# A two-block layer: the first round's four experts gathered in four column groups, the residual kept in column order, and the first expert's membership found ahead of the routing

## What is computed

```python
hn = rmsnorm(h, norm_ffn)
g_logits = tokens @ w_router_group;  g_idx = argmax(g_logits)            # 4 groups
e_sel = e_logits[g_idx];  top_v, top_i = lax.top_k(e_sel, 2)             # 2 of the group's 8 experts
gates = g_w * softmax(top_v)
ys = (silu(xb @ w_gate[e]) * (xb @ w_up[e])) @ w_down[e]                 # blocks of tokens of one expert
out = zeros.at[row_token].add(ys * row_gate)
h = h + out
```

## Time and profile before

| | us |
|---|---|
| median of 3 runs | 955.83 (955.31 to 957.48) |
| the profiled execution | 955.47 |
| its span, first to last instruction | 953.7 |
| PE / DVE / ACT / POOL busy | 782.6 / 465.6 / 318.0 / 99.0 |
| mean rate of the DMA | 301 GB/s |

### The profile page before, as it was taken

How to read it: one execution, slowest core, us unless ns; L and a number is a source line. 1 busy time by engine, 2 the same in 40 slices (tenths; PEclk the granted TensorE clock), 3 DMA queues, 4 the chain that set the end, 5 groups by cost and what they waited for, 6 DMA issues and landing times.

```text
span 953.7 us, 15749 instructions
## 1 busy us (share of the span) xinstructions
PE 782.6 (82%) x6548; PEld 601.2 (63%) x6548; DVE 465.6 (49%) x815; ACT 318.0 (33%) x525; POOL 99.0 (10%) x116
## 2 busy tenths in 40 slices
PE   5999999999984764747646566479999999999997
PEld 5988999777643432334423333236888888888885
DVE  6865849547421121201302012024968776766776
ACT  5764346732100000000000000003597554444444
POOL 3019673300000000000000000000000100000000
PEclk9999999999997887777979798779999999999999
DMA  9895243677999999999999999999975455555101
GB/s 318 272 354 177 90 177 145 259 311 294 415 427 428 426 429 426 427 427 429 428 429 427 428 429 427 429 428 388 363 266 178 155 189 201 183 177 177 45 1 45
DMA packets 72534, 286.67 MB, mean 301 GB/s; under 512 B 11882, under 2 KB 38688, under 8 KB 59936
## 3 DMA queue, kind: packets, MB, share of 16 engines
q1 hardware_dynamic: 71876, 284.81, 75.9%
q10 hardware_dynamic: 604, 1.10, 0.3%
HBM read 284.85 MB, written 1.05 MB: 300 GB/s over the span
## 4 chain that ended last, share of the span: by engine, by line
PE 54%; DMA 28%; issue 8%; DVE 4%; POOL 3%; ACT 2%; SPq 1%; POOLq 0%; DVEq 0%; ACTq 0%
DMA pair_d<-in_w_up_dram 22%; PE bank L664 11%; PE bank L613 11%; PE bank L629 9%; PE bank L2264 5%; PE bank L626 4%; PE bank L2288 4%; PE bank L641 4%; DMA ring<-in_w_in_dram 3%; DMA down_b<-in_w_down_dram 3%; PE bank L2230 1%; PE bank L2238 1%; PE bank L2095 1%; POOL seg_r L946 1%; ACT w_hi L583 1%
## 5 line engine op out<-in xcount | busy, mean ns | idle before, releaser
L593 DVE TENSOR_TENSOR w_lo<-ring,w_hi 128x1024 fp32r<-128x1024 f32 x135 | 174.7, 1294 | 101.9 <-ACT w_hi L583 101.5
L583 ACT ACTIVATE w_hi<-ring 128x1024 fp32r<-128x1024 f32 x136 | 144.2, 1060 | 178.3 <-PE bank L629 64.1
L613 PE MATMUL bank<-act_p,w_hi 128*128 128x256 f32 x736 | 137.7, 288 | 3.1 <-issue 2.0
L1776 DVE COPY y_e<-bank 32x256 f32<-32x256 f32 x64 | 27.2, 424 | 222.5 <-PE bank L2288 222.1
L629 PE MATMUL bank<-act_p,w_hi 128*128 128x512 f32 x344 | 119.3, 397 | 0.0
L613 PEld LDWEIGHTS bank<-act_p,w_hi 128*128 128x128 f32 x736 | 115.3, 192 | 6.0 <-issue 3.9
L1226 ACT ACTIVATE y_e<-bank 32x256 f32<-32x256 f32 x64 | 23.9, 374 | 256.7 <-PE bank L2288 256.4
L613 PE MATMUL bank<-act_p,w_lo 128*128 128x256 f32 x368 | 104.3, 283 | 0.0
L2288 PE MATMUL bank<-down_b,h_t 128*32 128x256 f32 x480 | 40.3, 493 | 74.6 <-issue 64.1
L664 PE MATMUL bank<-w_hi,act_q 128*128 128x512 f32 x288 | 90.6, 396 | 1.4 <-issue 0.8
L2264 PE MATMUL bank<-ring,moe 128*32 128x256 f32 x1472 | 84.0, 380 | 7.1 <-DVE moe L1739 6.7
(11 more groups left out here) (409 smaller groups left out, 1058.5 us busy)
## 6 DMA issues: line engine op xcount, KB each, us to landing
ring<-in_w_up_dram SPq DMA_DIRECT2D x24, 2048.0 KB, 34.6
ring<-in_w_gate_dram SPq DMA_DIRECT2D x23, 2048.0 KB, 30.2
down_a<-in_w_down_dram SPq DMA_DIRECT2D x15, 2048.0 KB, 25.9
down_b<-in_w_down_dram SPq DMA_DIRECT2D x15, 2048.0 KB, 25.8
ring<-in_w_in_dram SPq DMA_DIRECT2D x14, 2048.0 KB, 17.4
ring<-in_w_ffn_in_dram SPq DMA_DIRECT2D x22, 1024.0 KB, 7.6
pair_d<-in_w_gate_dram SPq DMA_DIRECT2D x8, 2048.0 KB, 30.0
pair_d<-in_w_up_dram SPq DMA_DIRECT2D x8, 2048.0 KB, 34.4
```

The lines of the kernel that those rows point to most:

```text
L583: nc.scalar.activation(parts(w_hi, g, view), view, ACT.Copy).then_inc(split_hi, 1)
L593: engine.tensor_tensor(parts(w_lo, g, view), view, h, ALU.subtract).then_inc(split_lo, 1)
L613: mm = nc.tensor.matmul(dst, parts(wt, g, grans[g][1])[:, k, :], a[:, x_part, k, :], start=(k == 0 and i == 0), stop=(k == KC - 1 and i == 2))
L1776: ins = nc.vector.tensor_copy(out_rows(e, j), down_rows(j))
```

## The change

Five edits, in the order in which they come in time. GpSimd's permuted copy of the input into `res` moves behind its masks and behind `gran_used` 1. The 16 grans of `w_out` are split through a view that reads the slot with a step of 8 elements (32 bytes) and writes in order (`eights`), so that the products come out in `res`'s order, and `add_res` becomes plain. VectorE finds first whether a token has expert 0 among its two (five small instructions), and TensorE ranks that alone, before the routing; the rest of the routing comes behind expert 0's one-hot matrix. Each of the experts 0 to 3 is gathered alone by `gather_alone`: the one-hot matrix is stationary, 32 columns wide, `res` moves, 256 columns in each of four column groups, eight products; `keep_alone` turns the result by a VectorE transpose of 32 x 32 blocks and scales it. `keep_running` is no longer called there, and `gate_up_pe(0, 1)` comes before the gathers of experts 2 and 3.

```diff
-    def row_grans(u, gains):
+    def row_grans(u, gains, eights=False):
         for j, gain in enumerate(gains):
-            grans.append((u, whole(u)[:, j * GR:(j + 1) * GR], gain))
+            view = whole(u)[:, j * GR:(j + 1) * GR]
+            grans.append((u, view.rearrange("p (q c) -> p c q", c=KC) if eights else view, gain))
...
-            r = natural(b, 64 * half, 64 * half + 64)
+            r = res[:, b, half * 512:(half + 1) * 512]
...
-            ins = nc.vector.tensor_tensor(r, r, in_eights(banks[2 * b + half][:, :]), ALU.add)
+            ins = nc.vector.tensor_tensor(r, r, banks[2 * b + half][:, :], ALU.add)
...
-        for b in range(TB):
-            nc.gpsimd.tensor_copy(natural(b), in_eights(x_tok[:, b, :]))
         mask(m_le[:, :], ALU.is_ge, 1, -1)
...
+        pool.wait_ge(gran_used, 1)
+        for b in range(TB):
+            ins = nc.gpsimd.tensor_copy(natural(b), in_eights(x_tok[:, b, :]))
+        ins.then_inc(const_ready, 1)
...
+        def keep_alone(e):
+            dve.wait_ge(xt_raw, e + 1)
+            if e:
+                dve.wait_ge(xt_kept, e)
+            turned_rows = gated[:, :, :].rearrange("p b t -> p (b t)")
+            link_dve(dve, nc.vector.transpose(turned_rows, bank[ALONE_BANK[e]][:, 0:2 * P]))
+            nc.vector.tensor_tensor(x_t[:, :, CAP * e:CAP * (e + 1)],
+                                    turned_rows.rearrange("p (c s) -> p c s", c=KC),
+                                    bcast(g_ffn[:, :].unsqueeze(2), [P, KC, CAP]), ALU.mult).then_inc(xt_kept, 1)
...
+        nc.vector.tensor_tensor(r8[:, 1, :, :], own, bcast(own[:, :, 0:1], [P, TB, EPG]), ALU.is_gt)
+        link_dve(dve, nc.vector.tensor_reduce(g_top, by_group(G_LOGIT), AX_X, ALU.max))
+        nc.vector.tensor_tensor(r8[:, 2, :, 1], by_group(G_LOGIT)[:, :, 0], g_top, ALU.is_ge)
+        link_dve(dve, nc.vector.tensor_reduce(r8[:, 2, :, 0], r8[:, 1, :, :], AX_X, ALU.add))
+        first = r8[:, 9, :, 2]
+        nc.vector.scalar_tensor_tensor(out=first, in0=r8[:, 2, :, 0], scalar=1.5, in1=r8[:, 2, :, 1], op0=ALU.is_le,
+                                       op1=ALU.mult).then_inc(member, 1)
...
+        keep_alone(0)
         nc.vector.tensor_reduce(g_at, by_group(G_AT), AX_X, ALU.min)
...
             if start:
-                keep_first(1)
                 gates()
+                keep_alone(1)
                 rounds()
+                keep_alone(2)
+                keep_alone(3)
                 gate_weights()
...
-        keep_running(4)
...
-        keep_running(2)
...
+        def gather_alone(e, which, o):
+            for b in range(TB):
+                row = res[:, b, :].rearrange("t (c p) -> t c p", c=KC)
+                for j in range(4):
+                    mm = nc.tensor.matmul(bank[ALONE_BANK[e]][CAP * j:CAP * (j + 1), 0:2 * P],
+                                          onehot[:, which, b, o:o + CAP], row[:, :, CAP * j:CAP * (j + 1)],
+                                          start=(b == 0), stop=(b == TB - 1))
+            mm.then_inc(xt_raw, 1)
...
             else:
+                gather_alone(0, 1, 0)
                 gate_up_apart(0)
+                ranks()
                 pe.wait_ge(built, 2)
-                gather_first(CAP, P - CAP, bank[5:7], 0)
+                gather_alone(1, 0, CAP)
+                pe.wait_ge(xt_kept, 2)
+                gate_up_pe(k, 1)
+                for e in range(2, 4):
+                    gather_alone(e, 0, CAP * e)
```

More of the change, by code:

```diff
@@ L252, in build @@
         row_grans(rows_unit(w["w_out"], ks[0], 4),
[L253 removed]
+                  [pcol("sc_norm", k - 8) if k >= 8 else pcol("ssd_norm", k) for k in ks], True)
     UA, GA = len(units), len(grans)
@@ L1654, in _ @@
         link_dve(dve, nc.vector.tensor_scalar(four(10), four(8), float(CAP), None, ALU.mult))
[L1655 to L1663, removed]
+        dve.wait_ge(rank_raw, 2)
         link_dve(dve, nc.vector.scalar_tensor_tensor(
@@ L1741, in keep_xt @@
                 bcast(g_ffn[:, 4 * half:4 * half + 4].unsqueeze(2), [P, 4, P]), ALU.mult).then_inc(xt_kept, 1)
[L1743 to L1757, removed]
         build_group(0)
-        keep_rest()
         def gate_up(x, e, first):
@@ L2211, in _, with ranks @@
             mm.then_inc(logits_raw, 1)
-        keep_running(4)
         pe.wait_ge(const_ready, 4)
         pe.wait_ge(member, 1)
-        nc.tensor.matmul(bank[5][:, 0:NE], m_lt[:, :], rt[:, 4, 0, :], start=True, stop=True)
-        for dst, last in ((bank[5][:, NE:2 * NE], m_lt), (bank[7][:, 0:NE], ones)):
-            nc.tensor.matmul(dst, ones[:, :], rt[:, 4, 0, :], start=True, stop=False)
-            nc.tensor.matmul(dst, last[:, :], rt[:, 4, 1, :], start=False, stop=True).then_inc(rank_raw, 1)
-        keep_running(2)
+        first = r8[:, 9, :, 2:3]
+        nc.tensor.matmul(bank[4][:, 0:1], m_lt[:, :], first[:, 0, :], start=True, stop=True)
+        nc.tensor.matmul(bank[4][:, 1:2], ones[:, :], first[:, 0, :], start=True, stop=False)
+        nc.tensor.matmul(bank[4][:, 1:2], m_lt[:, :], first[:, 1, :], start=False, stop=True).then_inc(rank_raw, 1)
+        def ranks():
+            pe.wait_ge(member, 3)
+            nc.tensor.matmul(bank[5][:, 0:NE], m_lt[:, :], rt[:, 4, 0, :], start=True, stop=True)
+            for dst, last in ((bank[5][:, NE:2 * NE], m_lt), (bank[7][:, 0:NE], ones)):
+                nc.tensor.matmul(dst, ones[:, :], rt[:, 4, 0, :], start=True, stop=False)
+                nc.tensor.matmul(dst, last[:, :], rt[:, 4, 1, :], start=False, stop=True).then_inc(rank_raw, 1)
         def tokens(b, c):
@@ L2232, in gather @@
             mm.then_inc(xt_raw, 1)
-        def gather_first(o, n, banks, which):
-            for c in range(KC):
-                for b in range(TB):
-                    mm = nc.tensor.matmul(banks[c // 4][:, (c % 4) * n:(c % 4 + 1) * n], tokens(b, c),
-                                          onehot[:, which, b, o:o + n], start=(b == 0), stop=(b == TB - 1))
-                if c % 4 == 3:
-                    mm.then_inc(xt_raw, 1)
+        def gather_alone(e, which, o):
+            for b in range(TB):
+                row = res[:, b, :].rearrange("t (c p) -> t c p", c=KC)
[4 more added lines that the diff above has]
+            mm.then_inc(xt_raw, 1)
         def gate_up_apart(e):
@@ L2336, in group_pe @@
             mm.then_inc(gmat_raw, 1)
-            if before is None:
+            if before is not None:
+                gate_up_pe(k, 1)
+            else:
                 pe.wait_ge(xt_kept, 4)
-            gate_up_pe(k, 1)
             down_pe(k, 0)
@@ L2352, in _ @@
         pe.wait_ge(member, 2)
-        gather_first(0, CAP, (bank[6], bank[1]), 1)
         group_pe(0, None)
```

24 lines of the change are left out of this document (16 added, 8 removed).

## The result

The changed kernel takes 972.95 us (median of 4 runs, 971.45 to 973.58) against 956.22 (955.31 to 957.48) of the kernel before on the same chip: a ratio of 1.0172, with a 95% interval of 1.0154 to 1.0190. By the ratio it is slower by 16.5 us; the forecast was 963.5 us, 8.0 slower. The profiled execution took 971.45 us, its span is 969.7 (before 955.47 and 953.7).

What follows compares the result with a forecast made beforehand. The prediction took the TensorE chain, then expert 5's issue that feeds the expert loads, as the bound. It summed +0.6 + 10.7 - 1.2 - 4.1 + 2.0 = +8.0 on 955.5 to 963.5 us, range 952.5 to 967.

Steps and rivals of the forecast that it cites:

- What bounds the kernel: Whole kernel: TensorE with some w_out splits, then routing with full buffers; the end moves with expert 5's issue at 245.32.
- the stream is never short again: Expert loads behind expert 5's pair: the rate stays over 420 GB/s, so the end moves as much as that issue.
- The start: Start and first grans: the moved GpSimd copy slows VectorE at gran 2 instead; +0.6 us, bounds -1.2 and +1.5.
- The split of `w_out`: Splits of w_out: the 32-byte step costs ScalarE and VectorE 0.8 us each per split; +5.9 and +4.8, together +10.7 us.
- add_res: Behind the last product of w_out: four plain instructions at 0.69 instead of 1.06 us; -1.2 us.
- Routing and gathers: Routing to expert 5's issue: it comes at 241.25 instead of 245.32; -4.1 us, bounds 0 and -5.
- The constant products and the clock: Routing: without these products TensorE idles and its clock falls, slowing the gate_up products; +2.0 us, bounds 0 and +4.
- The first down load: Behind expert 5's pair: moves from 247.04 to 249.3, hidden because the pair keeps the DMA busy for 9.8 us.
- Only VectorE pays: Rival, split of w_out: ScalarE's 1.15 us stays, the split adds +3.9 instead of 10.7; 956.9 us, chance 0.20.
- The free step: Rival, split of w_out: the step of 8 elements costs nothing, leaving -2.7 in all; 953 us, chance 0.26.
- The fourth: Rival, routing and start: clock falls twice and the moved copy is uncovered; +2.9, 966.5 us, chance 0.10 with the fifth.
- The fifth: Rival, routing: its second half holds expert 1, so expert 5's issue does not move; +4.1, 967.5 us, chance 0.10 with the fourth.

Runs made afterwards that it cites:

- copy_only: The kernel before with only GpSimd's copy of the tokens moved behind the first gran; 957.53 us, ratio 1.0003.
- pe_permuted: The changed kernel, but w_out is split contiguously and TensorE's products read the split copies with the 32-byte step; 992.37 us, ratio 1.0378.
- add_runs: The kernel before with add_res looping in runs along res, so only the bank is read with the step; 954.75 us, ratio 0.9983.
- split_only: The kernel before with only the permuted split of w_out and the plain add_res; 970.22 us, ratio 1.0148.
- more_products: The changed kernel with contiguous split, add_res in runs and constant products (3, 2, 2, 5, 2, 7) in TensorE's waits; 955.21 us, ratio 0.9989.
- const_back: The changed kernel with constant products put back into TensorE's waits of the routing; 970.74 us, ratio 1.0142.
- copy_at_start: As more_products, with GpSimd's copy of the tokens back at its old place; 956.39 us, ratio 0.9995.
- three_wide: As copy_at_start, but with only three constant products, of 512 columns, 6548 TensorE products in all; 954.89 us, ratio 0.9988.
- lo_stepped: The changed kernel, but only VectorE's half of the split reads w_out with the step, ScalarE reads contiguously; 963.07 us, ratio 1.0073.
- code_longer: add_runs with 18 one-column products more in TensorE's wait at the very start; 958.29 us, ratio 1.0020.
- step_sizes: The changed kernel with other steps in the split of w_out, two grans each, 1 to 512 elements; run once, 968.83 us.

## Why the prediction was wrong, step by step

**What bounds the kernel**: right in the main. The stretches, the hole and the issue that counts were read correctly; the issue moved by 14.6 us and the span by 16.0. The 1.4 between them goes against "the stream is never short again": behind expert 5's pair it falls to 254 GB/s (272 to 274 us). The prediction had named the DMA running dry there as a sign that it is wrong in its main point.

**The start** (+0.6): -0.1 at 60 us, and copy_only's 1.0003. L500 fell to 0.75 us and gran 2's subtraction rose, as forecast, to 1.87 (over 2 was expected); the sum of both is nothing that a run can tell.

**The split of `w_out`** (+10.7): this is the step that failed, by its size. The term was 10.7 us; the last product shows 14.9. Its mechanism held at each point: an engine that reads SBUF with the step pays, a bank is free for VectorE, ScalarE pays too, the chain alternates. Its argument that "the price lies in the memory and not in the engine" is borne out by pe_permuted, where TensorE pays as well, and by add_runs. But the price was taken from VectorE's rows (0.8) for both. VectorE's own was nearly right, 2.1 to 2.2 in the stretch (0.86 in the mean, with a bound of 0.8); ScalarE's is 1.13, above the bound of 0.9. And a gran of TensorE that starts from a wait takes 3.04 us, not 2.85. By the same sum with these terms: four `hi` at 1.13 and two `lo` at 0.86 are 6.2 instead of 4.8; two grans take 2.24 + 2.2 + 3.04 + 0.1 = 7.6 instead of 5.7, nine times 0.95 is 8.5 instead of 5.9. Together 14.7, where the last product shows 14.9. That they meet so closely is in part luck: from 190.00 us on the chain has four such steps of 7.5 to 7.6 us and one of 10.9 (197.53 to 208.44), in which VectorE makes an `act_q` product (L1544, 1.13 us) and a second subtraction on the chain. TensorE's work had covered both before, and the sum has no term for them.

**add_res** (-1.2): right, 686 ns each, and 29.2 to 28.0 in split_only.

**Routing and gathers** (-4.1): right at the issue. Without the clock's part it is 28.0 to 23.9, -4.1 (more_products).

**The constant products and the clock** (+2.0, bounds 0 and 4): under-sized. With the clock high the four stages took 1.07, 3.70, 1.07 and 3.66 (more_products); in the changed kernel they took 1.98, 5.04, 1.32 and 6.21. That is 5.0 us, above the upper bound. The two product stages lost 3.9 of it (1.3 and 2.6, near or just above the top of what the prediction allowed each). The other 1.2 lies in the two gathers, which the term left out.

**The first down load** ("the pair keeps the DMA busy, so that hides it"): right for the 8.0 us that it then stands behind expert 5's issue (const_back and copy_at_start need 51.2 us from expert 5's issue to expert 10's, before 51.1). With the low clock it is 9.5 behind, the stream has its second dip, and the same stretch takes 52.25: +1.2. The prediction did not add the clock's loss to it. That stretch by itself varies (52.3 in more_products, where the load is 8.0 behind), so the steadier count is from expert 5's issue to the end: 708.1 to 708.4 us in four kernels with the old gathers and 39 packets, 709.3 to 709.9 in the seven with the new gathers and no constant products. three_wide, whose load is 9.1 behind, has no dip and 708.1.

The account of the profiled execution at expert 10's issue: 14.9 - 1.2 - 4.1 + 5.0 + 1.2 = 15.8, and the trace shows 312.18 - 296.39 = 15.8. (The 1.2 is the measured difference of that stretch itself; the check lies in the 5.0, summed from the four stages, since the issue stands at 28.9 with the low clock and at 23.9 with the high one.) Of the 7.8 us that the 8.0 lacks, split and start together have 3.6 (14.9 for 11.3; the split alone 4.2), the clock 3.0 and the down load 1.2.

**Rivals.** Only VectorE pays: excluded, and with its true price it would have been some 963 (lo_stepped). The free step: excluded. The fourth had the clock's double fall, but not with this size. The fifth (expert 5's issue does not move) describes what is seen from the last product, 28.9 for 29.2, but not for its reason: with the clock high the issue comes at 23.9, so the second half of the routing does not hold it.

**What stays open.** Whether the clock falls in the routing differs between executions: it also fell in copy_only and code_longer, whose waits there are filled as in the kernel before. No run shows how often, and so a term of the clock read in one execution need not be that of the median. The price of the instruction fetch was not separated from the clock's in the totals. Nor was the remainder of the tail's 2.1 to 5.1 us, beyond the 1.4 of the stream in the window, followed further.

## What to carry to other kernels

A permuted view of float32 in SBUF made the instruction 1.6 to 2 times as long, on ScalarE and VectorE from a step of 16 bytes on, read or written, and on TensorE at the one step tried, 32 bytes read; put the permutation on the side of the bank, by the order of the loops, before moving it upstream. A price read from one engine's rows is a guess for another's; where both stand in series on the chain, size each. When work is added to or taken from an engine whose loop is long, compare the instruction packets of the two pages first: 57 against 39 went with a tail longer by 2.1 us or more here, as much as many of the edits that were tried.

## What was not expected of the hardware

- Instruction fetch can cost a kernel bound by DMA: with TensorE's list longer by 18 products ahead of the loop (36 records, 6548 to 6584), 18 more packets of 16 KB moved, 16 of them from 290 to 620 us, and the total was 3.5 us longer, the clock's part of it unknown.
- TensorE's product of 512 columns takes 0.43 us instead of 0.237 when its moving operand has a step of 32 bytes in SBUF, at the full granted clock.
- Two runs taken in turn (step of 2048 bytes) cost ScalarE 1.40 us per 1024 elements, against 2.06 to 2.27 at steps of 16 to 512 bytes (step_sizes).
- The clock fell to 0.5 while TensorE's records showed no gap, behind 32 products of 36 columns and in constant products of 512 columns. In code_longer the window from 222 to 226 us has it so (PE busy 4.00 of 4.00, granted clock 0.50):

```profile
222.00:226.00 4.00, 4.00 (x6) 1.61 (x5) 3.55 (x21) 0.00 (x0) 0.00 (x0) 0.50 1.01 434
```
